# First layer of a four-layer fp32 network: feature-major input and gate projections read in PSUM, head norms' squares moved to ScalarE, output projection started between attention steps

## The reference

```python
def rglru_group(h, w_in, conv_w, conv_b, w_r, b_r, w_i, b_i, lam):
    proj = h @ w_in
    u, gate, xq = jnp.split(proj, [D_LRU, 2 * D_LRU], axis=-1)       # 512 each
    u = causal_conv4(u, conv_w) + conv_b                             # by feature, over time
    ub = u.reshape(B, S, LRU_BLOCKS, LRU_BLK)
    r = jax.nn.sigmoid(einsum("bsnc,ncd->bsnd", ub, w_r) + b_r)
    i = jax.nn.sigmoid(einsum("bsnc,ncd->bsnd", ub, w_i) + b_i)
    log_a = -LRU_C * r * jax.nn.softplus(-lam)
    a = jnp.exp(log_a)
    b = jnp.sqrt(-jnp.expm1(2.0 * log_a)) * (i * u)
    _, hs = lax.associative_scan(_lin_combine, (a, b), axis=1)       # h[t] = a[t] h[t-1] + b[t]
    y = hs * jax.nn.gelu(gate, approximate=True)
    return y, xq

def memory_group(xq, mem, g_mem, w_kv, q_gain, k_gain):
    kv = rms_norm(mem, g_mem) @ w_kv                                 # k and v, 4 heads of 128
    q = rms_norm(xq by head, q_gain); k = rms_norm(k by head, k_gain)
    return softmax(q k^T / sqrt(128)) v

x = x + concatenate([y, y_mem]) @ w_out
x = x + square(relu(rms_norm(x) @ w_mlp_in)) @ w_mlp_out
```

## Time and profile before

| | |
|---|---|
| median of 3 runs | 1385.2 us (1383.5 to 1386.89) |
| the profiled execution | 1386.76 us, of which the span is 1384.7 us |
| TensorE busy | 1334.3 us, 96% of the span |
| VectorE busy | 877.8 us, 63% |
| ScalarE busy | 716.9 us, 52% |
| GpSimd busy | 128.9 us, 9% |
| chain that ended last | TensorE 81%, VectorE 11%, ScalarE 4% |
| TensorE by slices of 1/40 of the span | 6 8 6 9 9 9 ... 9 8 |

### The profile page before, as it was taken

The page is one execution under the profiler, slowest core; times in us unless marked ns, Lnnn a source line. Parts: engine busy times, 40 slices in busy tenths (PEclk is TensorE's granted clock), DMA queues, the critical chain, the costliest instruction groups (busy, mean ns, idle before and its releaser), DMA issues.

```text
span 1384.7 us, 18583 instructions
## 1 busy us (share of the span) xinstructions
PE 1334.3 (96%) x7229; PEld 1132.6 (82%) x7229; DVE 877.8 (63%) x1155; ACT 716.9 (52%) x1176; POOL 128.9 (9%) x163
## 2 busy tenths in 40 slices
PE   6869999999999999999999999999999999999998
PEld 5757888887888788888988778888889887788887
DVE  4884756566635656566765656666577756666665
ACT  6465544446665545456543445555465444555553
POOL 2120200004200300002101020000021010100000
PEclk9989999999999999999999999999999998999999
DMA  9432665655522565655541146555556221555551
GB/s 364 157 121 77 220 209 179 200 181 198 168 91 91 183 211 172 209 172 181 204 134 56 51 152 198 182 183 185 168 183 227 78 77 47 166 193 189 191 189 47
DMA packets 62328, 224.43 MB, mean 162 GB/s; under 512 B 7193, under 2 KB 7329, under 8 KB 62241
## 3 DMA queue, kind: packets, MB, share of 16 engines
q1 hardware_dynamic: 59616, 214.23, 46.4%
q0 software_dynamic: 1904, 6.82, 1.6%
q10 hardware_dynamic: 720, 2.19, 0.4%
HBM read 222.16 MB, written 1.05 MB: 161 GB/s over the span
## 4 chain that ended last, share of the span: by engine, by line
PE 81%; DVE 11%; ACT 4%; issue 2%; POOL 2%; DMA 0%; POOLq 0%; DVEq 0%; ACTq 0%
PE ps L323 15%; PE ps L277 15%; PE ps L282 15%; PE ps L281 15%; PE ps L327 8%; PE ps L433 3%; DVE wlo L1563 3%; PE ps L330 2%; PE ps L468 2%; PE ps L491 2%; PE ps L798 2%; PE ps L329 1%; DVE xn L1602 1%; ACT scr L1038 1%; ACT xn L1021 1%
## 5 line engine op out<-in xcount | busy, mean ns | idle before, releaser
L1563 DVE TENSOR_TENSOR wlo<-raw,whi 128x1024 fp32r<-128x1024 f32 (+1 forms) x402 | 479.4, 1213 | 266.5 <-ACT whi L984 264.7
L984 ACT ACTIVATE whi<-raw 128x1024 fp32r<-128x1024 f32 (+1 forms) x409 | 424.3, 1048 | 300.5 <-PE ps L323 178.5
L323 PE MATMUL ps<-XT,whi 128*128 128x512 f32 x896 | 318.6, 399 | 0.0
L327 PE MATMUL ps<-XT,wlo 128*128 128x256 f32 x896 | 251.6, 281 | 0.0
L323 PEld LDWEIGHTS ps<-XT,whi 128*128 128x128 f32 x896 | 168.4, 188 | 41.1
L277 PE MATMUL ps<-whi,HT_hi 128*128 128x512 f32 (+1 forms) x496 | 187.5, 378 | 1.6 <-DVE wlo L1563 1.1
L282 PE MATMUL ps<-whi,HT_lo 128*128 128x512 f32 (+1 forms) x496 | 186.3, 376 | 0.0
L281 PE MATMUL ps<-wlo,HT_hi 128*128 128x512 f32 (+1 forms) x496 | 186.1, 375 | 0.0
L327 PEld LDWEIGHTS ps<-XT,wlo 128*128 128x128 f32 x896 | 169.2, 189 | 1.2
L277 PE MATMUL ps<-whi,XT 128*128 128x512 f32 (+1 forms) x336 | 135.9, 405 | 10.1 <-DVE wlo L1563 7.7
L282 PE MATMUL ps<-whi,XT 128*128 128x512 f32 (+1 forms) x336 | 130.9, 390 | 0.0
(11 more groups left out here) (264 smaller groups left out, 1809.2 us busy)
## 6 DMA issues: line engine op xcount, KB each, us to landing
raw<-in_w_m SPq DMA_DIRECT2D x152, 512.0 KB, 4.1
raw<-in_w_n SPq DMA_DIRECT2D x108, 512.0 KB, 4.3
raw<-in_w_c SPq DMA_DIRECT2D x48, 512.0 KB, 4.1
raw<-in_w_o SPq DMA_DIRECT2D x32, 512.0 KB, 3.5
raw<-in_w_kv SPq DMA_DIRECT2D x16, 512.0 KB, 4.8
raw<-in_w_b SPq DMA_DIRECT2D x16, 512.0 KB, 3.4
raw<-in_w_w SPq DMA_DIRECT2D x16, 512.0 KB, 4.9
raw<-in_w_a SPq DMA_DIRECT2D x12, 512.0 KB, 7.3
```

The costliest lines, as they stand in the source:

```text
L323: m = pe.matmul(outs[f][:, :], hi[:, j, at], both, start=(k == 0), stop=False)
L327: pe.matmul(outs[f][:, 0:T], lo[:, j, at], XT[0][:, k, :], start=False, stop=False)
L984: act.activation(whi[:, g % NSPLIT, 0:w], raw[:, g % NRAW, 0:w], ACT.Copy).then_inc(split_hi, 1)
L1563: dve.tensor_tensor(wlo[:, g % NSPLIT, 0:w], raw[:, g % NRAW, 0:w], whi[:, g % NSPLIT, 0:w].bitcast(F32), ALU.subtract).then_inc(split_lo, 1)
```

## The change

The first layer's order is rewritten. `xq0` is computed first (units 0 to 3). `u` (4 to 7) and `gate` (8 to 11) are computed by feature: the weight tile is the stationary operand, and 24 matmuls of 256 columns a unit replace 12 of 512. They stay in banks 2 to 5 and are read there, so `u` and `gate` are no longer copied, turned and copied again. `mk` follows (12 to 15), then `mv` (16 to 19). The squares for the head norms are made by ScalarE from the banks (`rows_in`), and GpSimd only makes the roots. VectorE scales the keys, straight from their banks, and the product of the two head gains is applied as a column while ScalarE copies the turned keys. The sigmoids are folded into the following operations. The first two units of the output projection stand between the attention's third and fourth steps' work.

```diff
+            block_by_token("xq0", "w_a", 1, tok(XT), [0, 1], after_norm(0))
+            feature_pairs("u", (2, 3), [a["w_a"][u] for u in range(4)], {2: lambda: turn_norm(1, 0), 3: lambda: turn_norm(1, 1)})
+            feature_pairs("gate", (4, 5), [a["w_a"][8 + u] for u in range(4)],
+                          {0: lambda: mem_queries(0, (0,)), 1: lambda: mem_queries(0, (1,))})
...
-            for g, banks in ((0, (2, 3)), (1, (4, 5))):
+            for g, banks in ((0, (2, 3)), (1, (6, 7))):
...
+            mem_kv(0, "mk", [0, 1])
+            mem_kv(0, "mv", [2, 3], {2: lambda: mem_keys(0)})
+            mem_ready(0)
+            out_left = out_first(0, "w_o0")
...
+            attend(["ma0"], {"ma0": mem_spec(0)}, {(2, 2): lambda: (pe.wait_ge(ev("ylo"), 1), next(out_left)),
+                                                   (3, 2): lambda: next(out_left)})
             for tt in range(TT):
...
+                mem_rows(0, tt)
+                next(out_left)
+            for _ in out_left:
+                pass
+            out_second(0, "w_o0", 2, "mo0")
```

ScalarE:

```diff
+            rows_in("xq0", hrow[:, :, :].rearrange("p a b -> p (a b)"), slot(3, 1024))
...
+            for f in range(4):
+                ps = full(f"u.{f // 2}")
+                act.activation(slot(0, 1024)[:, f * T:(f + 1) * T], ps[:, (f % 2) * T:(f % 2 + 1) * T], ACT.Identity,
+                               bias=cb[:, f:f + 1], scale=cw[:, 4 * f + 3:4 * f + 4]).then_inc(ev("tap"), 1)
+            mem_turned(0, 0)
+            for half in range(2):
+                ps = full(f"gate.{half}")
+                act.activation(slot(10, 1024)[:, half * BLK:(half + 1) * BLK], ps[:, :], ACT.Square).then_inc(ev("gsq"), 1)
...
+            act.wait_ge(ev("gcub"), 2)
+            act.activation(slot(10, 1024), slot(10, 1024), ACT.Tanh,
+                           scale=0.044715 * 0.7978845608028654).then_inc(ev("gtanh"), 1)
+            splits(fills["mk0.0"].pos)
             act.wait_ge(ev("b2"), 1)
...
+            act.activation(slot(8, 1024), slot(8, 1024), ACT.Sqrt, scale=-0.25).then_inc(ev("bsq"), 1)
+            rows_in("mk0", hrow[:, :, :].rearrange("p a b -> p (a b)"), None)
...
+            soft(["ma0"], {1: rglru_hi})
```

VectorE:

```diff
-            for tt in range(TT):
-                norm_lo(1, tt, MX)
...
+            gain_column(sm("mgcol", 2)[:, 0:1], P, rg("xaq0"), rg("xak0"))
+            fox_sums(1, sm("cq", 16)[:, 0:8], hq(8, P).rearrange("p n d -> p (n d)"), P)
+            norm_lo(1, 0, MX)
             dve.wait_ge(ev("lamexp"), 1)
             log1p(l4, z, w4, t4)
...
+            norm_lo(1, 1, MX)
...
+                    m = dve.scalar_tensor_tensor(uc[:, f * T + s:(f + 1) * T], PS[fills[f"u.{f // 2}"].bank][:, c:c + T - s],
+                                                 cw[:, 4 * f + 3 - s:4 * f + 4 - s], uc[:, f * T + s:(f + 1) * T],
+                                                 ALU.mult, ALU.add)
...
+                splits(fills["u.1"].pos + AHEAD + s - 1)
+            dve.memset(sm("one", 1), 1.0).then_inc(ev("conv"), 1)
+            splits(fills["gate.1"].pos)
...
+            step(dve.scalar_tensor_tensor(uc, ti, 1.0, uc, ALU.add, ALU.mult))
             dve.wait_ge(ev("decay"), 1)
...
             step(dve.scalar_tensor_tensor(om, decay, 1.0, th, ALU.add, ALU.mult))
             dve.scalar_tensor_tensor(s8, decay, 1.0, om, ALU.add, ALU.mult).then_inc(ev("b2"), 1)
...
+            splits(fills["mk0.0"].pos)
             dve.wait_ge(ev("bsq"), 1)
             step(dve.tensor_tensor(uc, uc, s8, ALU.mult))
...
+            splits(fills["mk0.1"].pos + AHEAD)
+            fox_sums(2, sm("rk8", 8), hq(8, P).rearrange("p n d -> p (n d)"), P)
+            splits(fills["mv0.0"].pos)
...
+            gelu()
...
+            soft(["ma0"], {1: rglru_lo, 3: lambda: rows_out(["ma0"], "ma0", 0, xn[:, 0, 512:1024])})
+            rows_out(["ma0"], "ma0", 1, xn[:, 1, 512:1024])
```

GpSimd:

```diff
-            def squares(src, groups, hd, wait):
...
-            mem_norms(0, 0)
+            roots([("cq", 16, 8, P, P ** -0.5), ("rk8", 8, 8, P, 1.0)])
```

More of the change, by code:

```diff
@@ L537, in mem_keys @@
             def mem_keys(i):
-                pe.wait_ge(ev("mkn"), i + 1)
+                if i == 0:
+                    for tt in range(TT):
+                        read_out(f"mk0.{tt}")
+                else:
+                    pe.wait_ge(ev("mkn"), 1)
                 for tt in range(TT):
@@ L1152, in _ @@
                     free(f"rg{g}.{half}", m)
[L1154 to L1162 removed]
+            act.wait_ge(bank_free[fills["rg0.1"].bank], fills["rg0.1"].turn)
@@ L1625, in norm_x @@
                 norm_lo(k, 1, XT)
-            def hsums(dst, src, after=None):
-                if after:
-                    splits(fills[after].pos + AHEAD)
-                st["hs"] = st.get("hs", 0) + 1
-                dve.wait_ge(ev("sq"), st["hs"])
-                dve.tensor_reduce(dst, src, AX.X, ALU.add).then_inc(ev("hsum"), 1)
             def hq(n, hd):
@@ L1772, in _ @@
                     free(name, m)
-            splits(fills["u.1"].pos + AHEAD)
+            splits(fills["xq0.1"].pos + AHEAD)
             for tt in range(TT):
@@ L1815, in _ @@
-            hsums(sm("cqm", 8), hq(8, P), "xq0.1")
-            hsums(sm("rk8", 8), hq(8, P), "mk0.1")
-            r, ig, s8, om = slot(1, 1024), slot(2, 1024), slot(8, 1024), slot(7, 1024)
-            for g in range(2):
-                for half in range(2):
-                    nm = fills[f"rg{g}.{half}"]
-                    splits(nm.pos + AHEAD)
-                    dve.wait_ge(bank_free[nm.bank], nm.turn)
-            dve.tensor_scalar(r, r, 0.5, 0.5, ALU.mult, ALU.add).then_inc(ev("rgate"), 1)
@@ new lines, in _ @@
+            dve.memset(sm("one", 1), 1.0).then_inc(ev("conv"), 1)
+            splits(fills["gate.1"].pos)
+            gt, s8, om, ti = slot(10, 1024), slot(8, 1024), slot(4, 1024), slot(2, 1024)
+            decay, th = slot(7, 1024), slot(11, 1024)
+            for half in range(2):
+                at = slice(half * BLK, (half + 1) * BLK)
+                ps = full(f"gate.{half}")
+                dve.wait_ge(ev("gsq"), half + 1)
+                dve.scalar_tensor_tensor(gt[:, at], gt[:, at], 1.0 / 0.044715, ps[:, :], ALU.add, ALU.mult).then_inc(ev("gcub"), 1)
@@ L1836, in _ @@
             dve.wait_ge(ev("bsq"), 1)
             step(dve.tensor_tensor(uc, uc, s8, ALU.mult))
-            for tt in range(TT):
-                splits(fills[f"gateT.{tt}"].pos + AHEAD)
-                dve.wait_ge(bank_free[fills[f"gateT.{tt}"].bank], fills[f"gateT.{tt}"].turn)
-            gt = slot(10, 1024)
-            step(dve.tensor_tensor(s8, gt, gt, ALU.mult))
-            step(dve.tensor_scalar(s8, s8, 0.044715 * 0.7978845608028654, 0.7978845608028654, ALU.mult, ALU.add))
-            dve.tensor_tensor(s8, s8, gt, ALU.mult).then_inc(ev("gcub"), 1)
@@ new lines, in _, with gelu @@
+            splits(fills["mv0.0"].pos)
+            for tt in range(TT):
+                ps = full(f"mk0.{tt}")
+                at = slice(tt * BLK, (tt + 1) * BLK)
+                m = scaled(slot(5, 1024)[:, at].rearrange("p (n d) -> p n d", d=P), ps[:, :], sm("rk8", 8)[:, 4 * tt:4 * tt + 4],
+                           2, P)
+                free(f"mk0.{tt}", m)
+            def gelu():
+                dve.wait_ge(ev("gtanh"), 1)
+                for half in range(2):
+                    at = slice(half * BLK, (half + 1) * BLK)
+                    ps = full(f"gate.{half}", 0)
+                    free(f"gate.{half}", dve.scalar_tensor_tensor(gt[:, at], gt[:, at], 1.0, ps[:, :], ALU.add, ALU.mult), True)
+                dve.scalar_tensor_tensor(om, om, 0.5, gt, ALU.mult, ALU.mult).then_inc(ev("yrow"), 1)
```

256 lines of the change are left out of this document (86 added, 170 removed).

## The result

The change made the kernel 0.8% faster: 1375.01 us in the median (1373.46 to 1375.35, 4 runs) against 1385.53 of before in the same comparison, a ratio of 0.9923 [0.9906, 0.994]. That is 10.5 us. The profiled execution took 1375.35 us, its span 1373.2, 11.5 less than before's.

A forecast was written before the change was run, and what follows sets the result against it. TensorE, busy 96% of the span, was taken as the bound, with VectorE's order setting its first-layer waits. 10.4 us won at full clock less 4.8 left 5.6: from 1385.2 to 1379.6, given as 1380, range 1375.5 to 1384.5.

The forecast's parts named there:

- wait for unit 7: First layer, before the gates: TensorE, done at 38.4, waits 1.6 us for VectorE's split, ready at 40.0.
- at bank 6: Before the gates: the first turn of `xq0` waits 2.1 us until VectorE gives bank 6 back at 49.0.
- 3.3 behind the scans: Between gates and first scores: TensorE waits 3.3 us for unit 16's split, which VectorE makes only after the scans.
- waits in the attention: First layer's attention: TensorE waits 1.2, 3.1 and 2.3 us while ScalarE and VectorE set the pace.
- third piece: From the first scores to unit 22, one turn included: 22.2 us against 22.4 in the old kernel, 0.1 won.
- the rival of slow taps: Convolution taps reading a bank take 0.8 us, adding 3.4 before the gates and a 2.5 clock fall: 1385.5; chance 0.05.
- the deductions: Taken off 10.4 us: 2.5 for clock behind the scans' wait, 1.3 in the attention, 1.0 for hand-overs and tails.
- Behind unit 22 the orders are as before: After the first layer's unit 22 the forecast took the remaining work as unchanged and put no gain or loss there.
- The full clock holds: Clock stays full through the second piece or the attention: 8.1 to 9.4 us won, 1376 to 1377; chance 0.15.
- Clock lost at every longer wait: Falls of 2.5 us each at `xq0`'s turn, the scans and the attention: 1.9 won, 1383.3; chance 0.18.
- the slower case: Half clock behind all five first-layer waits from 1.6 us up costs 12.5: 3.1 slower, 1388.3; chance 0.05.
- The units between the steps bring nothing: Output projection units placed between the attention's steps win nothing; already counted so, no chance of its own.

The follow-up runs named there:

- a_same: The changed kernel, unchanged, run again; 1374.5 us in the median, ratio 0.9931 to the old kernel.
- a_busy: The changed kernel with 18 unread transposes on TensorE ahead of the third attention step's turn, filling its wait there; 1377.36 us, ratio 0.9942.
- a_delay84: The changed kernel with 84 more unread transposes in the first MLP's turns as pure delay; 1387.43 us, ratio 1.0017.
- a_early: The changed kernel with VectorE's splits of units 20 and 21 done ahead of the attention's first maximum; 1373.25 us, ratio 0.9921.
- a_no_inter: The changed kernel with units 20 and 21 behind the attention instead of between its last steps; 1375.26 us, ratio 0.994.
- a_delay16: The changed kernel with 16 more unread transposes in the first MLP's turns as pure delay; 1377.88 us, ratio 0.9947.
- a_bank: The changed kernel with VectorE's second memory turn, which frees bank 6, ahead of the logarithm's small operations; 1378.76 us, ratio 0.9949.
- a_pool_late: The changed kernel with three unread products of 128x1024 on GpSimd from 88 us on; 1380.21 us, ratio 0.9956.
- b_busy: The old kernel with 92 unread transposes filling five TensorE waits in the first layer; 1381.84 us, ratio 0.9973.
- b_same: The old kernel, unchanged, run again; 1385.2 us in the median, ratio 1.0004.
- a_busy16: The changed kernel with 24 unread transposes on TensorE in the wait of 3.0 us ahead of unit 16; 1377.43 us, ratio 0.9943.
- three edits: The changed kernel with, singly, unit 16's split ahead of the scans, bank 6 freed earlier, units 20 and 21 split earlier: 1374.81, 1378.76, 1373.25 us; together 1369.1.

## Why the prediction was wrong

**The schedule was right.** At full clock the prediction put unit 22 at 110.9; after's 112.72 less the 1.6 of unit 20 is 111.1. Its steps one by one: wait for unit 7 1.6 (1.15 measured), at bank 6 2.1 (1.71), gates' end 61.9 (61.49), no wait for unit 15 (0.39), 3.3 behind the scans (3.04), first scores 89.05 (89.41), waits in the attention 1.2, 3.1 and 2.3 (1.35, 2.68 and 2.15), third piece 22.2 with the turn (23.3 - 1.6 + 0.36 = 22.1). Taps 0.52 (0.51), so the rival of slow taps falls; products behind the decay 1.23 each (1.22 and 1.23).

**The steps that failed are the deductions.** The prediction's words are "the wait of 3.3 us will let the clock fall, as 2.59 with 0.77 ahead did, 2.5", half of 2.5 for the attention, and 1.0 for tails: 10.4 - 4.8. In the profile of after the wait of 3.04 cost nothing of the clock, the attention cost 1.6, and 10.4 - 1.6 - 8.6 = 0.2 is left for the tails. "Will" was wrong, and so was the size: the 2.5 came from unit 16 of before, behind whose wait the clock stood at 0.50 for 6.8 us; the falls of after's kind in this place lasted 3.4. Nine profiled executions here have that wait of 3.0 with nothing on TensorE in it: after, a_same, a_busy, a_delay84 and a_early show 1.00 in the window 73 to 81, a_no_inter, a_delay16, a_bank and a_pool_late 0.79. So it falls in some executions and not in others, and where it does, it costs 14.5 - 12.9 = 1.6 us up to the first scores and not 2.5. An expected charge of 0.7 there, and 1.6 in the attention, would have given 7 to 8 us.

**The other part lies where I had put 0.** "Behind unit 22 the orders are as before" is true of the orders, and the rest still took 2.9 us less in the profiled pair (the turn counted), since it ran at 0.50 for less time. By the whole-run clock: before's comparison sets have a mean of 0.9856 to 0.9864, 38 to 40 us at 0.50, after's two sets 0.9912 and 0.9908, 24 to 25. That is some 14 us x 0.33 = 4.6 of the 10.5 us, an estimate, and 5 to 6 remain for the schedule (in the profiled first layer 8.6 - 4.3 + 1.6 = 5.9). The prediction had 10.4 - 4.3 (what the clock cost before's first layer) - 1.0 = 5.1 for the schedule and 4.3 - 3.8 = 0.5 for the clock. **The mis-sized term is the clock's: 0.5 forecast, 4.6 measured.** In the two profiles 4.3 - 1.6 = 2.7 of it lie in the first layer; the other 2, by the same estimate, are in layers that the change does not touch.

**Rivals.** "The full clock holds" (8.1 to 9.4 won, chance 0.15) was nearest, for the first layer: 8.6. "Clock lost at every longer wait" and the slower case fall. "The units between the steps bring nothing" holds in the new order (a_no_inter). No rival priced a clock behind unit 22 that differs from before's.

**What stays open.** After's executions have a clock of 0.990 or more in 8 of 10, before's in 10 of 74. Most of that lies in the first layer, since b_busy has it in 10 of 12. What decides at which of the later places the clock falls is not settled: the profiles have 13.5 to 30.6 us at 0.50 behind unit 22, before and b_same, one program, 27.3 and 20.4, and a_busy16, with after's code there, the high clock in 2 of 6. The delays of 1.7 and 9.1 us did not settle whether the place in time matters; with four to twelve runs a kernel, chance is not excluded either.

The page cited in the prediction, the Trainium skill's "TensorE: Matmul & The Clock Gate", says in its section "What's actually happening" that the clock is set by how busy the array has been recently, and that throttled is its default state. The prediction read from it that each new wait is a risk. The nine profiles above agree with that, a risk and no certainty: at one and the same wait of 3.04 us the clock fell in four and stayed in five.

## What to carry to other kernels

Work out the schedule at full clock first, and state the clock as a term of its own, with both signs: what the old kernel lost to it comes back, and a new wait loses it again only in a part of the executions. Compare medians of few runs only together with their mean granted clock; here 0.005 of it was 14 us at half clock and 4.6 us of time, as much as the schedule's gain. When a change moves work off GpSimd, look for passes of VectorE that stood beside it: 3 us of 6 came from there. And a small edit is judged by its own stretch of the profile: three edits that won 0.8, 1.9 and 2.1 us there won 0.2, lost 3.8 and won 1.8 in the median, and together won 5.4 to 5.9.
